# Stacking the sample tokens' split keys and values: six transfers per head in place of eight identity matmuls and two ScalarE copies

## The reference

```
s     = einsum('bhjk,bhsk->bhjs', qc, kc) * w_intra
num   = einsum('bhjs,bhsd->bhjd', s, vc) + w_inter * einsum('bhvk,bhjk->bhjv', C, qc)
C_new = decay * C + einsum('bhs,bhsv,bhsk->bhvk', w_s, vc, kc)
n_new = decay * n + einsum('bhs,bhsk->bhk', w_s, kc)
```

## Time and profile before

| | us |
|---|---|
| median of 3 runs | 941.18 |
| lowest, highest | 940.92, 941.48 |
| span of the profiled execution | 940.7 |
| TensorE busy in it | 928.3 (99%) |
| VectorE | 772.2 (82%) |
| ScalarE | 464.4 (49%) |
| GpSimd | 106.7 (11%) |

### The profile page before, as it was taken

How to read it: one execution, slowest core, us unless ns; L and a number is a source line. 1 busy time by engine, 2 the same in 40 slices (tenths; PEclk the granted TensorE clock), 3 DMA queues, 4 the chain that set the end, 5 groups by cost and what they waited for, 6 DMA issues and landing times. The chain is left out here.

```text
span 940.7 us, 18449 instructions
## 1 busy us (share of the span) xinstructions
PE 928.3 (99%) x6833; PEld 907.8 (96%) x6833; DVE 772.2 (82%) x1231; ACT 464.4 (49%) x684; POOL 106.7 (11%) x110
## 2 busy tenths in 40 slices
PE   8999999999999999999999999999999999999996
PEld 8999999999999999999999999999999999999995
DVE  6899985988698869876455569999888999889997
ACT  6654452445336324634833345456545555455664
POOL 3011330042006001500231000000000000000001
PEclk9999999999999999999999999999999999999998
DMA  6245216211620352042342222233222223232122
GB/s 219 68 150 198 69 57 224 90 45 56 246 90 23 134 191 90 23 150 87 117 140 68 89 73 84 90 108 106 102 90 91 90 68 113 90 116 109 46 91 100
DMA packets 22460, 98.56 MB, mean 105 GB/s; under 512 B 2929, under 2 KB 5122, under 8 KB 17909
## 3 DMA queue, kind: packets, MB, share of 16 engines
q1 hardware_dynamic: 19576, 77.13, 24.9%
q0 software_dynamic: 1984, 19.72, 5.7%
q10 hardware_dynamic: 832, 0.88, 0.3%
HBM read 85.28 MB, written 12.44 MB: 104 GB/s over the span
## 5 line engine op out<-in xcount | busy, mean ns | idle before, releaser
L1301 PE MATMUL ps<-h_hi,w_hi 128*128 128x288 f32 x896 | 193.7, 298 | 0.0
L1301 PE MATMUL ps<-h_lo,w_hi 128*128 128x288 f32 x896 | 191.7, 295 | 0.0
L1301 PE MATMUL ps<-h_hi,w_lo 128*128 128x288 f32 x896 | 191.4, 295 | 0.0
L793 ACT ACTIVATE w_hi<-raw 128x1024 fp32r<-128x1024 f32 x76 | 80.4, 1058 | 177.4 <-PE ps L1301 174.2
L1301 PEld LDWEIGHTS ps<-h_hi,w_hi 128*128 128x128 f32 x896 | 143.5, 189 | 1.3 <-issue 0.6
L1301 PEld LDWEIGHTS ps<-h_hi,w_lo 128*128 128x128 f32 x896 | 144.3, 189 | 0.0
L1301 PEld LDWEIGHTS ps<-h_lo,w_hi 128*128 128x128 f32 x896 | 144.2, 188 | 0.0
L1692 DVE TENSOR_TENSOR w_lo<-raw,w_hi 128x1024 fp32r<-128x1024 f32 x76 | 94.2, 1240 | 48.9 <-ACT w_hi L793 48.8
L1917 DVE SCALAR_TENSOR_TENSOR conv<-a_p,vec,conv x120 | 97.6, 813 | 0.2
L1569 PE MATMUL ps<-cols_b,late 128*128 128x288 f32 x432 | 62.8, 295 | 0.1
L1569 PE MATMUL ps<-cols_a,main 128*128 128x288 f32 x432 | 62.9, 295 | 0.0
(11 more groups left out here) (362 smaller groups left out, 1857.3 us busy)
## 6 DMA issues: line engine op xcount, KB each, us to landing
raw<-w_head_in SPq DMA_DIRECT2D x40, 512.0 KB, 3.5
raw<-w_fp_in SPq DMA_DIRECT2D x18, 1024.0 KB, 4.9
cs<-st_c_in POOLq DMA_DIRECT2D x4, 2048.0 KB, 9.6
c_s_out<-cs POOLq DMA_DIRECT2D x4, 2048.0 KB, 7.7
raw<-w_fo_in SPq DMA_DIRECT2D x8, 1024.0 KB, 4.9
x<-xT_in SPq DMA_DIRECT2D x16, 288.0 KB, 4.1
raw<-w_cgcv_in SPq DMA_DIRECT2D x8, 512.0 KB, 3.6
raw<-w_ga_in SPq DMA_DIRECT2D x8, 512.0 KB, 3.5
```

The lines of the kernel that those rows point to most:

```text
L793: act.activation(w_hi[:, s, :], raw[:, s, :], ACT.Copy).then_inc(hi_ready, 1)
L1301: last = pe.matmul(ps[:, 2 * s + b, 0:HALF], wt[:, w, k * P:k * P + P], src[:, k, b * HALF:b * HALF + HALF], start=(k == 0 and wt is w_hi ...
```

## The change

The split parts now lie side by side in one tile `kvs` (64 partitions by four parts of 256). ScalarE no longer copies banks; after `inter` it issues six transfers from `kvs` to `stk`, three for each group of 32 tokens, and each group has a semaphore of its own. GpSimd and TensorE wait for these. The two PSUM uses go out of the list, and with them the identity pieces, their clearing on GpSimd and the four small copies that filled them.

```diff
-        kv_hi = nc.alloc_sbuf_tensor_at("kv_hi", [P, 2 * HD], F32R, offset=hf_base)
-        kv_lo = nc.alloc_sbuf_tensor_at("kv_lo", [P, 2 * HD], F32R, offset=hf_base + 4 * 2 * HD)
+        kvs = nc.alloc_sbuf_tensor_at("kvs", [P, 4, HD], F32R, offset=hf_base)
+        K_HI, K_LO, V_HI, V_LO = range(4)
+        stacked = (kvs[:, K_HI:V_LO + 1:V_LO - K_HI, :], kvs[:, K_HI:V_HI + 1:V_HI - K_HI, :], kvs[:, K_LO:V_HI + 1, :])
...
-            steps.on(pool.memset(place3[:, :, :, :].rearrange("p g r t -> p (g r t)").bitcast(F32), 0.0))
...
                 for g in range(2):
-                    pool.wait_ge(act_read, h * ACT_USES + (START + READER[:K_USE + g].count("act") + 1))
+                    pool.wait_ge(stk_placed[g], h * 48 + 48)
                     pool.tensor_tensor(wvs[0:3 * GT, g * SG:g * SG + SG, :],
...
                 act.activation(inter[0:TS, :], bank(I_USE)[0:TS, 0:HD + SB], ACT.Copy).then_inc(act_read, 1)
+
+                act.wait_ge(kvsplit_ready, h * 2 + 2)
                 for g in range(2):
-                    use(K_USE + g)
-                    act.activation(stk[0:3 * GT, g, :], bank(K_USE + g)[0:3 * GT, :], ACT.Copy).then_inc(act_read, 1)
+                    for r, src in enumerate(stacked):
+                        act.dma_start(stk[r * GT:r * GT + GT, g, :].rearrange("p (c v) -> p c v", c=2).bitcast(F32),
+                                      src[g * GT:g * GT + GT, :, :].bitcast(F32)).then_inc(stk_placed[g], 16)
 
                 act.wait_ge(dve_read, h * DVE_USES + (START + 5))
                 act.activation(w2_hi[:, :], wts[:, 0:W_OFF[NB]], ACT.Copy).then_inc(pvhi_ready, 1)
...
-                pe.wait_ge(place_ready, 4)
-                pe.wait_ge(kvsplit_ready, h * 2 + 2)
-                for g in range(2):
-                    use(K_USE + g)
-                    for c, (of_hi, of_lo) in enumerate(((2, 0), (1, 3))):
-                        for first, src in ((of_hi, kv_hi), (of_lo, kv_lo)):
-                            last = pe.matmul(bank(K_USE + g)[0:3 * GT, c * HD:c * HD + HD],
-                                             place3[0:TS, g, first:first + 3, :].rearrange("p r t -> p (r t)"),
-                                             src[0:TS, c * HD:c * HD + HD], start=(src is kv_hi), stop=(src is kv_lo))
-                    last.then_inc(attn_ready, 1)
                 head_unit(7)
...
+                for g in range(2):
+                    pe.wait_ge(stk_placed[g], h * 48 + 48)
                 pe.wait_ge(wvs_ready, h * 2 + 2)
...
-            for g in range(2):
-                for r in (2, 3):
-                    dve.tensor_copy(place3[0:TS, g, r, :], ident[0:TS, g * GT:g * GT + GT]).then_inc(place_ready, 1)
```

More of the change, by code:

```diff
@@ L89 @@
 I_G = [G_STEP * _t for _t in range(NB)] + [1]
-S_USE, T_USE, I_USE, K_USE, PV_USE, CP_USE, CS_USE, N_USE, HT_USE = 0, 5, 10, 11, 13, 18, 20, 28, 29
-USES = 32
-READER = ["dve"] * 5 + ["act"] * (5 + 1 + 2 + 5 + 2) + ["dve"] * (8 + 1 + 3)
+S_USE, T_USE, I_USE, PV_USE, CP_USE, CS_USE, N_USE, HT_USE = 0, 5, 10, 11, 16, 18, 26, 27
+USES = 30
+READER = ["dve"] * 5 + ["act"] * (5 + 1 + 5 + 2) + ["dve"] * (8 + 1 + 3)
 ACT_USES, DVE_USES = READER.count("act"), READER.count("dve")
@@ L188, in half_of @@
     return KH if is_in(i) else GROUPS[ROUNDS[i][1]] // 2
-POOL_SET = 16
+POOL_SET = 15
 DVE_HEAD_STEPS = 89
@@ L269, in build @@
         rows_d = nc.dram_tensor("rows_d", (NH * NI, P), F32, kind="Internal").ap()
-        place3 = sb("place3", [2, 6, GT], F32R)
         cols = sb("cols", [NI, NH])
@@ L487, in build @@
         wv_ready = sem("wv_ready")
-        place_ready = sem("placement_ready")
+        stk_placed = [sem(f"samples_kv_stacked{g}") for g in range(2)]
         kvsplit_ready = sem("samples_kv_split")
@@ L1963, in _ @@
                 k5, v5 = kvn[0:TS, NB, 0:HD], kvn[0:TS, NB, HD:2 * HD]
-                steps.on(dve.tensor_copy(kv_hi[0:TS, 0:HD], k5))
-                steps.on(dve.tensor_scalar(kv_hi[0:TS, HD:2 * HD], v5, w5, None, ALU.mult))
+                steps.on(dve.tensor_copy(kvs[0:TS, K_HI, :], k5))
+                steps.on(dve.tensor_scalar(kvs[0:TS, V_HI, :], v5, w5, None, ALU.mult))
                 steps.settle()
-                dve.tensor_tensor(kv_lo[0:TS, 0:HD], k5, kv_hi[0:TS, 0:HD].bitcast(F32), ALU.subtract)\
+                dve.tensor_tensor(kvs[0:TS, K_LO, :], k5, kvs[0:TS, K_HI, :].bitcast(F32), ALU.subtract)\
                     .then_inc(kvsplit_ready, 1)
-                dve.scalar_tensor_tensor(kv_lo[0:TS, HD:2 * HD], v5, w5, kv_hi[0:TS, HD:2 * HD].bitcast(F32),
+                dve.scalar_tensor_tensor(kvs[0:TS, V_LO, :], v5, w5, kvs[0:TS, V_HI, :].bitcast(F32),
                                          ALU.mult, ALU.subtract).then_inc(kvsplit_ready, 1)
@@ L1987, in _ @@
                 lo_of(7)
-                dve.wait_ge(act_read, h * ACT_USES + (START + 13))
+                dve.wait_ge(act_read, h * ACT_USES + (START + 11))
                 wi = hcol(I_WI, TS)
```

## The result

| | before | after |
|---|---|---|
| median, us | 941.33 (4 runs) | 956.76 (4 runs: 955.68 to 957.17) |
| ratio after/before | | 1.0156, 95% interval 1.0142 to 1.0171 |
| span of the profiled execution | 940.7 | 954.2 |

A timed run is 1.5 us longer than its own span (955.68 against 954.2 for the profiled one here, and the same in every later run). So the profiled execution before, with its span of 940.7, belongs to a run of some 942.2 us, 0.9 over the median; the 0.5 us given ahead of the prediction mixed two different executions.

The account below looks back on a forecast made before the run. TensorE is full in the head loop, with no slack for VectorE's kvn_lo at the first PV matmul. That chain ends 1.58 us later per head: 941.18 + 4 x 1.58 (+6.3) = 947.5 us, range 943.8 to 951.9.

Parts of the forecast that it names:

- the 0.5 us given ahead of the prediction: Offset between profiled span and run median: the median was taken as 0.5 us above the span.
- No slack at PV, so nothing is gained ahead of it: First PV matmul: starts 0.15 us behind kvn_lo, so TensorE's gains ahead are lost unless VectorE's chain shortens.
- Removed: 1.0 us a head: TensorE ahead of unit 7: eight matmuls per head go, taking 1.0 us off each head, 4 us in all.
- GpSimd and VectorE take turns by whole instructions: wvs, w2_lo, wvs, kvn_lo: four pieces run in turn, 6.07 us from the first wvs to kvn_lo's end.
- Six issues at 0.43, 2.6 us: ScalarE between inter and w2_hi: six transfer issues take 2.6 us (2.3 to 3.8), to 125.0.
- The end of the chain moves by what the first wvs moves: GpSimd's first wvs starts 1.58 us later, so kvn_lo's end moves by +1.58 us per head.
- The clock: Rival: TensorE's new idle time drops PV matmuls to 1.2 GHz, costing 18 us on top, 965; chance 0.05.
- Nothing behind PV gives back or takes more: After PV: TensorE was full so has no slack to give back, and nothing more is late; no added cost.
- the saving stands: Rival: wvs runs beside or after VectorE's work, PV level with TensorE, 1.0 us per head gained, 937.1; chance 0.10.
- My bound with all three terms at their worst: Upper case with first issue's start, issue pitch and landing time all at their longest: 956.7 us.

Follow-up runs that it names:

- e6: Kernel before, with each head's eight stacking matmuls cut to two of 32 columns (stk holds stale numbers): 941.18 us, ratio 0.9992.
- e8: Kernel before, whole, with GpSimd's wvs held back until VectorE has made kvn_lo: 942.65 us, ratio 1.0007.
- e5: Changed kernel with the six transfers issued by SP in place of ScalarE, wvs starting as soon as they have landed: 939.37 us, ratio 0.9972.
- e9: Changed kernel with the second group's three issues moved behind v_hi, the first three left ahead of w2_hi: 945.75 us, ratio 1.0048.
- e2: Changed kernel with one more wait on GpSimd, so wvs starts only when w2_lo and kvn_lo are made: 951.78 us, ratio 1.0107.
- e3: Changed kernel with the six issues moved behind w2_hi and v_hi on ScalarE: 939.89 us, ratio 0.9983.
- e1: Changed kernel with 24 throwaway matmuls per head filling most of TensorE's idle time before the wait for kvn_lo: 949.71 us, ratio 1.0082.
- e4: Changed kernel with the six transfers issued by SP in place of ScalarE and wvs held back until kvn_lo is made: 938.47 us, ratio 0.9966.

## Why the prediction was wrong

The direction held, and the place: TensorE waits for `kvn_lo` ahead of PV, four times. The forecast was +6.3 us and +15.4 was measured, outside the range. Two steps failed, the time of an issue and the clock.

- *No slack at PV, so nothing is gained ahead of it*: right, shown by e6 (no gain from the cut matmuls, 0.75 us of new waiting a head) and e8.
- *Removed: 1.0 us a head*: 1.11.
- *GpSimd and VectorE take turns by whole instructions*: right. e5 and e9 show it with the other order, and the second with PV to 0.04 us.
- *Six issues at 0.43, 2.6 us*: **mis-sized.** They take 0.75 for the first and 0.62 for the others, 3.98 us. I took the pitch from stores out of SBUF; the form was not in the trace, and the upper bound of 0.63, which I had from one row, was the right one. The third issue came 0.57 us later than I put it, the landing took 2.0 in place of 1.9: `wvs` began 2.24 us later than before against the reference point, not 1.58.
- *The end of the chain moves by what the first wvs moves*: near in the number, wrong as the cause. The issues held `w2_hi` by 3.40 us, so `w2_lo` came only when `wvs` ended and took 1.49, not 2.2; that both chains ended within 0.1 us of each other is chance (two issues, a landing and 1.89 us on one side, six issues and 1.28 on the other), and it is why the sum by `wvs` still comes out. The hold on `w2_hi` makes PV late by itself: with the collision gone, 1.63 us of waiting stay (e2). The landing alone doesn't: with the hold gone and `wvs` as late, no wait at PV is left (e3). The collision adds its 1.7 us on top of the hold. PV moved by 2.40 us in head 0, 2.3 in the mean, where I had 1.58: 0.7 to 0.8 a head, some 3 us in all.
- *The clock*: **the step that put the result out of the range.** The sum has it at nothing. I had it as a rival with 0.05, leaning on one idle stretch of 2.2 us at the start of the kernel. With the true issue time the idle time is 3.3 us, not 2.6, and the clock fell in every head. e1 prices it at 7.05 us, nearly half of the result; my own price for it, 18, was far over. With the issues as they are and the clock up, e1 measured 949.71, which lies in the range. Two terms hung together here: a cost mis-sized by 0.7 us a head pushed the wait to where it cost another 1.4 to 1.8.
- *Nothing behind PV gives back or takes more*: true of the changed kernel, whose list has no such wait. Experiments that bring PV forward meet two more bounds, ScalarE's copy of the first PV block and VectorE's reading of the state updates' banks, both within 1 us of the first. The rival "the saving stands" would have been right only with the issues out of the way of `w2_hi`, and then for 3.2 of the 4.1 us (e4; 1.6 in e3).

In sum: +6.3 forecast, +3 for the chain, +5.4 (profiled) to 7 (timed) for the clock: 14.7 to 16.3, against 15.4 measured. My bound with all three terms at their worst, 956.7, stands beside the measured 956.76 by luck: it had a landing of 3.1 us, which took 2.0, and no clock. The forecast also added 0.5 us between a span and a median, which are 1.5 apart for one and the same run; since it moved a median by a difference, this changes nothing.

## What to carry to other kernels

A transfer costs its issuing engine time in its program order; ask what stands behind the issues on that engine before asking how fast the bytes land, and give them to an engine with nothing behind them. Where TensorE is full, price a new wait twice, once for its length and once for the clock behind it, and work the second out at the long end of the first. A producer with no slack hides others right behind it: taking one away gives what the next allows.

## What the runs showed of the hardware

- A transfer from 32 partitions of SBUF to 32 others, 64 KB, takes its issuer 0.62 us on ScalarE and 0.60 on SP (0.75 for the first of a row), whether its source lies in one run of 2 KB or two of 1 KB; SP's weight loads of 512 KB take 0.33. It lands in 2.0 us. What makes the issue longer is open; no run varied its size or its number of partitions.
- Idle stretches of TensorE of 1.4 to 1.7 us (e2, e9) left the granted clock up; stretches of 3.3 to 3.4 us (the changed kernel, four of four) were followed, 0.3 to 0.4 us after work began again, by 3.4 us at 1.2 GHz. Idle time isn't all that counts: at the end of the kernel before, the clock fell between 932 and 934 though the longest wait near it was 0.8 us; no run looked into that.
- VectorE's instructions with two SBUF inputs and GpSimd's shut each other out whole, also where VectorE holds and GpSimd waits (e9: the first `wvs` 3.21 us in place of 1.89 behind a `w2_lo` of 1.49). The Trainium skill, page GPSIMD Engine Reference, section Key points, says that the two contend there; that whole instructions wait is what these rows add.
- Unit matmuls ahead of the reference point of head 0 came in pairs 0.267 us apart in the profiled runs before, of e4 and of e6, and 0.261 in those of the changed kernel and all others, about 1 us in all. From 30 to 60 us behind it they are 0.267 apart in every run. I have no cause for it.
